# Two combinations moved between weight pieces, and the last layer norm's work split anew over three engines

## The reference

```python
h = layer_norm(DEEPNORM_ALPHA * h + mix, ln1_g[l], ln1_b[l])
ffn = grouped_moe(h, w_router, b_router, w1[l], w3[l], w2[l])
h = layer_norm(DEEPNORM_ALPHA * h + ffn, ln2_g[l], ln2_b[l])
# in grouped_moe, for each of 32 experts and the tokens routed to it (2 experts per token):
hb = jax.nn.silu(xb @ w1[e]) * (xb @ w3[e])
return hb @ w2[e]                       # then weighted by the gate and summed per token
```

## Time and profile before

| | |
|---|---|
| median of 3 runs | 1280.0 us (1279.83 to 1280.03) |
| profiled execution, its own time | 1280.34 us |
| its span | 1278.5 us |
| TensorE busy | 1232.3 us, 96% |
| VectorE, ScalarE, GpSimd busy | 445.9, 320.2, 7.1 us |
| HBM read | 469.14 MB, 369 GB/s over the span with the writes |

### The profile page before, as it was taken

The page is one execution under the profiler, slowest core; times in us unless marked ns, Lnnn a source line. Parts: engine busy times, 40 slices in busy tenths (PEclk is TensorE's granted clock), DMA queues, the critical chain, the costliest instruction groups (busy, mean ns, idle before and its releaser), DMA issues.

```text
span 1278.5 us, 15203 instructions
## 1 busy us (share of the span) xinstructions
PE 1232.3 (96%) x6605; PEld 704.4 (55%) x6605; DVE 445.9 (35%) x636; ACT 320.2 (25%) x546; POOL 7.1 (1%) x17
## 2 busy tenths in 40 slices
PE   6999999999999999999999989989999999999987
PEld 6989888988744444444443434434444444444532
DVE  7889996855410203133130202111120211111026
ACT  5443333533322211111211111111112111111212
POOL 1000000000000000000000000000000000000000
PEclk9999999999999999999999999999999999999998
DMA  9655555696999999999999999999999999999995
GB/s 307 216 187 192 168 194 183 237 383 222 360 384 422 418 420 427 426 426 429 428 432 429 434 428 429 434 429 426 435 429 425 427 428 428 427 427 429 423 403 226
DMA packets 66998, 472.26 MB, mean 369 GB/s; under 512 B 7290, under 2 KB 7874, under 8 KB 41074
## 3 DMA queue, kind: packets, MB, share of 16 engines
q1 hardware_dynamic: 66498, 470.47, 90.5%
q10 hardware_dynamic: 432, 0.79, 0.2%
HBM read 469.14 MB, written 2.10 MB: 369 GB/s over the span
## 4 chain that ended last, share of the span: by engine, by line
PE 81%; DMA 16%; DVE 2%; issue 0%; ACT 0%; SPq 0%; DVEq 0%; ACTq 0%
PE psum L962 32%; DMA places<-in_w_dram 15%; PE psum L1007 9%; PE psum L736 9%; PE psum L884 7%; PE psum L707 7%; PE psum L663 6%; PE psum L666 3%; PE psum L920 2%; PE psum L921 2%; PE psum L1042 1%; PE psum L949 1%; DMA area_a<-in_x_dram 1%; PE psum L857 1%; DVE area_b L2040 0%; PE psum L985 0%
## 5 line engine op out<-in xcount | busy, mean ns | idle before, releaser
L962 PE MATMUL psum<-places,area_c 128*64 128x512 f32 x2048 | 457.9, 600 | 22.7 <-DMA places<-in_w_dram 22.7
L962 PEld LDWEIGHTS psum<-places,area_c 128*64 128x64 f32 x2048 | 146.6, 138 | 305.0 <-issue 300.6
L1007 PE MATMUL psum<-places,area_d 128*64 128x512 f32 x928 | 202.8, 594 | 1.4 <-DMA places<-in_w_dram 1.4
L1339 ACT ACTIVATE area_c<-psum,gain 128x128 f32<-128x128 f32 x256 | 96.5, 457 | 294.4 <-PE psum L884 294.4
L1910 DVE TENSOR_TENSOR area_a<-area_a,psum 128x512 f32<-128x512 f32 x56 | 38.3, 685 | 357.9 <-PE psum L921 357.9
L1506 DVE TENSOR_TENSOR w_low<-places,w_high 128x2048 fp32r<-128x2048 f32 x55 | 125.9, 2289 | 60.5 <-ACT w_high L1173 60.4
L1173 ACT ACTIVATE w_high<-places 128x2048 fp32r<-128x2048 f32 x55 | 105.3, 1915 | 139.8 <-PE psum L666 53.2
L1007 PEld LDWEIGHTS psum<-places,area_d 128*64 128x64 f32 x928 | 65.7, 137 | 127.8 <-issue 124.4
L884 PE MATMUL psum<-one_hot,area_b 128*128 128x128 f32 x1024 | 124.9, 278 | 0.3 <-DVE one_hot L1836 0.3
L884 PEld LDWEIGHTS psum<-one_hot,area_b 128*128 128x128 f32 x1024 | 118.0, 192 | 12.9 <-issue 12.2
L1894 DVE TENSOR_TENSOR y_low<-psum,y_high 128x512 fp32r<-128x512 f32 x64 | 42.7, 687 | 231.3 <-ACT y_high L1348 231.3
(11 more groups left out here) (219 smaller groups left out, 734.0 us busy)
## 6 DMA issues: line engine op xcount, KB each, us to landing
places<-in_w_dram SPq DMA_DIRECT2D x97, 2048.0 KB, 23.6
places<-in_w_dram SPq DMA_DIRECT2D x27, 4096.0 KB, 21.0
places<-in_w_dram SPq DMA_DIRECT2D x70, 1024.0 KB, 10.6
places<-in_w_in_dram SPq DMA_DIRECT2D x40, 1024.0 KB, 5.1
places<-in_w_out_dram SPq DMA_DIRECT2D x16, 1024.0 KB, 5.2
places<-in_w_dram SPq DMA_DIRECT2D x8, 512.0 KB, 19.1
places<-in_w_dram SPq DMA_DIRECT2D x16, 256.0 KB, 9.3
area_a<-in_x_dram SPq DMA_DIRECT2D x4, 512.0 KB, 6.1
```

Of the source, the lines that this page charges most:

```text
L962: mm = pe.matmul(psum[i * CAP:(i + 1) * CAP, j // UNITS, :], gathered[:, kk, i * CAP:(i + 1) * CAP], w[i][:, k, :], start=kk == 0, stop=kk ...
L1007: mm = pe.matmul(psum[i * CAP:(i + 1) * CAP, 4 + c, :], hidden_t[:, f, i * CAP:(i + 1) * CAP], w[i][:, c, :], start=f == 0, stop=f == FT - 1)
L1339: ins = act.activation(gathered[:, k, :], psum[:, 2 + g % 2, k % 4 * P:(k % 4 + 1) * P], ACT.Identity, scale=gain[:, 0, k:k + 1], bias=gai ...
```

## The change

Two things, both at the end of the kernel. First, step 14's combination of block 2 moves from behind piece j = 7 to behind j = 5, and that of block 3 to behind j = 6; VectorE's additions of these two blocks move ahead of its last `hide`. Second, in the final norm: the first operation on the first block (t = 0, 1024 columns) is split into two of 512, and the reciprocal with the scale stands between them; and the fourth block (t = 1, columns 1024 to 1535) goes from VectorE to POOL, as three operations, of which the first waits for the scale. The last store waits for POOL's `pool_out` in place of the fourth `y_out`.

```diff
@@ SyncE, stores
-                    sp.wait_ge(y_out, TT * h + t + 1)
+                    if (h, t) == (1, TT - 1):
+                        sp.wait_ge(pool_out, 1)
+                    else:
+                        sp.wait_ge(y_out, TT * h + t + 1)
@@ POOL, at the end
+            block_cols = slice(D // 2, D - CW)
+            pool.wait_ge(scale_ready, TT * 3)
+            pool.wait_ge(s_g2, 16 * 2)
+            dst = area_b[:, TT - 1, block_cols]
+            nc.gpsimd.tensor_scalar(dst, area_a[:, TT - 1, block_cols], rstd[:, TT - 1, 2:3], rstd[:, TT - 1, 3:4],
+                                    ALU.mult, ALU.add).then_inc(pool_step, 1)
+            pool.wait_ge(pool_step, 1)
+            nc.gpsimd.tensor_tensor(dst, dst, ln2_scale[:, block_cols], ALU.mult).then_inc(pool_step, 1)
+            pool.wait_ge(pool_step, 2)
+            nc.gpsimd.tensor_tensor(dst, dst, ln2_shift[:, block_cols], ALU.add).then_inc(pool_out, 1)
@@ TensorE, last_two_steps
-                    if j in (UNITS, 2 * UNITS - 1):
-                        first = 0 if j == UNITS else NC // 2
-                        combine(a, first)
-                        combine(a, first + 1)
+                    if j == UNITS:
+                        combine(a, 0)
+                        combine(a, 1)
+                    elif j < 2 * UNITS - 1:
+                        combine(a, j - UNITS + 1)
@@ VectorE, last step
+                    for i in range(2):
+                        add_combined(it - 1, 2 + i, COMBINED[i])
                 hide(it, it == PAIRS - 1)
-            for i in range(2):
-                add_combined(PAIRS - 2, 2 + i, COMBINED[i])
@@ VectorE, final norm
-            for m in range(2 * TT):
+            for m in range(2 * TT - 1):
                 h, t = divmod(m, TT)
                 cols = slice(0, D // 2) if h == 0 else slice(D // 2, D - CW)
-                link(v.scalar_tensor_tensor(out=area_b[:, t, cols], in0=area_a[:, t, cols], scalar=mv[:, t, 0:1],
-                                            in1=ln2_scale[:, cols], op0=ALU.subtract, op1=ALU.mult))
+                pieces = (slice(0, CW), slice(CW, 2 * CW)) if m == 0 else (cols,)
+                for piece in pieces:
+                    link(v.scalar_tensor_tensor(out=area_b[:, t, piece], in0=area_a[:, t, piece], scalar=mv[:, t, 0:1],
+                                                in1=ln2_scale[:, piece], op0=ALU.subtract, op1=ALU.mult))
+                    if m == 0 and piece.start == 0:
+                        norm_scale(6, slice(0, TT))
                 if m == 0:
-                    norm_scale(6, slice(0, TT))
                     dve.wait_ge(scale_ready, TT * 3)
```

More of the change, by code:

```diff
@@ L288, in hybrid_layer @@
         comb_ready, comb_added = sem("combined_ready"), sem("combined_added")
+        pool_step, pool_out = sem("last_block_step"), sem("last_block_out")
         y_out, first_added = sem("y_out"), sem("last_combined_first_tile_added")
```

## The result

| | before | changed |
|---|---|---|
| median | 1279.79 us (22 runs) | 1281.30 us (22 runs) |
| profiled execution | 1280.34 us, span 1278.5 | 1281.33 us, span 1279.4 |
| variance to the span's end | 1278.5 - 1266.89 = 11.61 | 1279.4 - 1265.45 = 13.95 |

"Variance to the span's end" is the time from the start of VectorE's operation on both tiles' variance, the last one ahead of the final norm (line 1451 before, 1467 after), to the end of the span. It leaves out all that differs between executions ahead of the norm.

A forecast was written before the change was run, and what follows sets the result against it. The prediction took TensorE, busy 96% of the span, as the bound, with time to win only in its waits or behind its last product. 0.75 (combinations) + 0.05 (stores) = 0.8 off 1280.0 gave 1279.2 us; range 1278.4 to 1282.8.

The forecast's parts named there:

- POOL beside VectorE: Final norm: whether both engines' SBUF reads exclude each other, which the trace couldn't settle; one overlap showed no hold.
- the first rival: Final norm: POOL and VectorE take turns, store 3 is 3.1 to 4.0 late, +2.3 in all, 1282.3; chance 0.30.
- Combinations, 0.75: Last w3 pieces: 2.26 of work goes into 2.01 of gaps, so w2's first product comes 0.75 earlier, at 1243.8.
- Rival 3: Last w3 pieces: gaps before pieces 6 and 7 are DMA waits and may be absent, giving 1280.2; chance 0.05.
- Is it kept?: From w2's first product to the norm: no later wait for weights or ln2 rows, so the whole 0.75 stays.
- POOL's own lengths: POOL's block in the final norm: operations of 0.75, 1.27 and 1.27, with hand-overs 3.4, at most 4.2.
- Split operation: Final norm's first block: scale 0.54 earlier for ScalarE, TensorE and POOL, second operation 0.12 later on VectorE.
- The stores: Kernel's end: store 4 is issued 0.35 behind store 3, queues, lands some 3.5 after issue; gain 0.05.
- Rival 2: Final norm: POOL waits for VectorE and gets in only at 1274.13, +1.3 in all, 1281.3; chance 0.13.

The follow-up runs named there:

- e2: The kernel before with only the new norm (split operation and POOL's block), combinations as before: 1282.27 us, ratio 1.0016.
- e4: As e3, with POOL doing the same three operations on unused scratch tiles, no result depending on them: 1281.49 us, ratio 1.0018.
- e5: As e4, with three POOL memsets of 128x2048 on an unused scratch tile in place of the three operations: 1280.28 us, ratio 1.0002.
- e9: As e4, with four POOL tensor_tensor operations on scratch data after its tensor_scalar instead of two: 1283.77 us, ratio 1.003.
- e12: As e4, with VectorE's first operation of the second, third and fourth block a tensor_scalar with one SBUF input: 1280.05 us, one execution.
- e3: The changed kernel with both parts, but the fourth block stays on VectorE and POOL does nothing in the norm: 1279.99 us, ratio 1.0005.
- e1: The kernel before with only the two moved combinations and their additions ahead of the hide, norm as before: 1279.51 us, ratio 0.9996.
- e8: The kernel before with only block 2's combination moved, behind piece 6; block 3's stays behind piece 7: 1278.66 us, ratio 0.999.
- e6: As e3, with the last store in two of 256 KB, the last 512 columns first, then VectorE's block: 1279.37 us, ratio 1.0.

## Why the prediction was wrong

The step that failed is the paragraph on POOL beside VectorE, and with it the choice of the forecast (0.45) over the first rival (0.30). I costed POOL's block at nothing as it had 3 us of cover before its result was wanted. The cover was real: POOL was done at 1272.46, and SyncE wanted it at 1275.4. What it cost lay elsewhere, on VectorE: 2.29 in the trace, 2.35 in e2's median. The evidence that I took against it, one overlap of 0.55 with an operation on 8 partitions, was too thin. It shows no hold, and no run here says why. e4 shows the cause with the same operations on other tiles, e5 that POOL's writing isn't it, e9 that it scales with their number.

The rule of the Trainium skill (SBUF — State Buffer, Who interferes with whom) spoke against the change and was right in kind: the one that comes later waits for the other. The words "fully blocks", which stand there for VectorE's faster forms, fit here to within a little: a tensor_tensor of 1.27 holds VectorE for 0.88 to 1.00 and not for the 1.27 that I took for rival 1, whose 3.1 therefore came out at 2.3. The same section of the Trainium skill also says that VectorE's tensor_scalar contends in its faster form; e12's 1.75 agrees with it.

Point by point:

- **Combinations, 0.75.** For the trace at hand it was exact: piece 4 at 1223.32 plus the 20.48 from piece 4 to the first product in the changed trace gives 1243.80, and 1243.8 was forecast. (The changed trace's product stands at 1243.11 as its piece 4 started 0.69 earlier, and nothing of the change lies ahead of piece 4; over the three traces of before it starts at 1223.32 to 1224.19.) But the term was mis-sized as a mean: the gaps before pieces 6 and 7 are a matter of each execution, and over four of them it is worth 0.23. Rival 3 had this mechanism, at a chance of 0.05, and was set aside because the change touches no load. It needs no change of a load: the gaps differ between executions of one kernel.
- **Is it kept?** Right: from w2's first product to the variance it is 22.34 before and after (1266.89 - 1244.55, 1265.45 - 1243.11).
- **POOL's own lengths.** Forecast 0.75, 1.27 and 1.27; they show 1.20, 2.11 and 2.13, each with a wait in it. The first was issued at 1266.85, while a VectorE operation ran to 1267.41, and from there to its end it is 0.64, about half of the 1.20 of twice the columns. So a POOL operation of some 0.64 (an estimate) held VectorE for 0.40.
- **Split operation.** Right: the reciprocal came 0.78 after the norm's first operation began, and not 1.31; the cost on VectorE was forecast at 0.12, e3 shows 0.14 in all.
- **The stores.** Right: store 4 was issued some 0.4 behind store 3 and landed 3.5 after. The block's leaving VectorE is worth next to nothing: e4 has it on VectorE and ends 0.11 later behind the variance (14.06 against 13.95).
- **Rival 2** (POOL waits until VectorE is through) named the measured total of 1281.3, by a mechanism that the trace doesn't show. Right number, wrong way: 2.3 lost in turns, less what the combinations give.

The sum by what the runs show: +2.3 for the norm (e2), -0.4 for the combinations (e1), 1.9, against 1.5 between the medians and an interval from 1.0 to 2.6.

## What to carry to other kernels

Work given to POOL isn't free because POOL is idle: if it reads SBUF while VectorE works through SBUF tiles on the critical path, they can take turns, and VectorE pays most of each POOL operation (0.9 to 1.0 of 1.27 here). It did so for VectorE's two-input operations and for its tensor_scalar, and not for the batch statistics, so look at the lengths of your own operations beside each other before you count on cover. Before you move work into gaps on the critical engine, look at the gaps in several executions: what is left by a DMA in one is gone in the next, while a wait that the order of the work makes (here for the hide behind piece 7) is there every time, and one piece of other work that fits into it costs next to nothing (e8: 5.48 against 5.43). And where stores already lie end to end, neither an earlier last operand nor a smaller last store brought the end forward here.

## What the runs showed of the hardware

- A POOL tensor_tensor on 128x512 holds a VectorE operation by 0.88 to 1.00, whether VectorE's own takes 1.28 or 0.75; the tensor_scalar on 128x512 held one by 0.40. Three memsets of 1.8 each held none.
- POOL waits as well: 2.11 and 2.13 for what took 1.27 in the kernel's first part.
- A POOL tensor_scalar on 128x1024 beside VectorE's batch statistics of one SBUF tile (before, 10.01 to 11.21): 1.20 and 0.68 to 0.70, no hold.
- VectorE's tensor_scalar with one SBUF input takes 0.53 for 512 columns, against 0.75 for the two-input form, and is held too (1.75 where some 0.84 is estimated for 1024 columns).
- Cutting the last 512 KB store in two (e6) left its data's end where it was and made the landing 0.4 later.
- From piece 5 to piece 7 it is 7.85, 8.53, 9.17 and 9.18 in four executions of the same order of work, as the waits for the DMAs of pieces 6 and 7 differ.
